# A mixture-of-experts loop, written out, with its matrix products in another order and its weights loaded in runs of 8 KB

## The chip, the cores and the metric

The kernel runs on one core of a Trainium2 chip. The time is device microseconds (us) of one execution, and the median of several runs is compared.

## What is computed

One layer of a hybrid model over two groups of 128 tokens (256 tokens of 1024 features in all, everything in float32). A token mixer (attention, a gated recurrence, a gated MLP) comes first; then every token goes through 4 of 32 experts:

```python
logits = hf @ wr + br;  top_v, top_i = top_k(logits, 4);  gates = softmax(top_v)
def swiglu_expert(xb, wg, bg, wu, bu, wd, bd):
    gate = minimum(xb @ wg + bg, 7.0)
    up = clip(xb @ wu + bu, -7.0, 7.0)
    glu = gate * sigmoid(1.702 * gate)
    return ((up + 1.0) * glu) @ wd + bd
out[t] = sum over the 4 experts e of token t: gates[t, e] * swiglu_expert(h[t], e)
```

Each expert has three 1024 x 1024 matrices (gate, up, down), 12.6 MB together, so the loop over the 32 experts reads 403 MB of weights once.

## The kernel before

It is written with explicit engines and semaphores: each engine runs its own list of instructions, and waits stand where the author wrote them.

**Weights.** SyncE loads all large weights through one ring of 12 slots of 1 MB (`ring`, each 128 partitions x 2048 floats). A slot is loaded again when TensorE has counted it as used (`chunks_used`). An expert is 12 chunks, four to a matrix, so the ring holds just one expert. A chunk is 256 rows of a matrix; partition p holds rows p and 128 + p of it, that is two runs of 4 KB. `load_expert` stands in a hardware loop over the experts.

**One expert on TensorE** (the loop at line 1480, two experts to a turn). `product(B[0], 0, ...)` opens the bank with the bias (line 1424, 32 rows of `pick` against `mbias`) and adds 16 pairs of matmuls (line 1431): the stationary operand is 64 token slots, the moving one 512 columns of weights, and the two halves of the 1024 columns go to the two halves of one bank. `combine` (line 1441) adds the previous expert's stored rows `ysb`, scaled by `gT`, into four banks. `spread` (line 1406) broadcasts the next expert's ranks and gates over the partitions for VectorE, which makes `gT` of them (lines 998, 1001). `product(B[1], 1, ...)` is the up product. `gather` (line 1415) multiplies the token rows by a 0/1 matrix `Ptok` into the 64 slots of the next expert. `down` transposes the activations (line 1454) and waits for ScalarE's copy of them (line 623) before the down product (line 1431 too, from `k_pool`).

**VectorE** clips the gate (`gate_step`, line 1005), prepares the next expert's routing (`route`, `slot_gates`), and after the up product makes the activation (`up_step`, lines 1009 to 1013). **ScalarE**, in this order: the sigmoid (line 619), the copy of the gathered tokens out of its bank (line 615), the copy of the transposed activations (line 623), the copy of the down product's rows (line 625).

Ahead of the loop stand the router and, on TensorE, matmuls that only keep it at work (`keep_clock`, line 1134), the first spread and gather, and `open_sums` (line 1463), which starts the four result banks with the gates times the down bias. The normed rows are made on VectorE at lines 934 and 940 and transposed at line 1368.

An expert has 64 slots. If more than 64 tokens choose it, later rounds follow behind a branch; a list of them is made at line 1471.

Of the kernel before, what the change touches and what calls it, by code (L numbers as in the profile page):

```python
# [20 lines left out]
ALU = mybir.AluOpType  # L21
# [37 lines left out]
AT_MOE = AT_MODG2 + 4  # L59
WOUT = [2, 3, 0, 1]  # L60
# [4 lines left out]
C_SLOTCOL = C_SLOTROW + CAP  # L65
C_THR, C_E, C_OFF = C_SLOTCOL + 1, C_SLOTCOL + 2, C_SLOTCOL + 3
C_IOTA = C_SLOTCOL + 4
# [4 lines left out]
def shape_constants():  # L72
# [9 lines left out]
    f[:, C_SLOTROW:C_SLOTROW + CAP] = np.arange(1, CAP + 1)  # L82
    f[:, C_SLOTCOL] = i % CAP + 1
# [18 lines left out]
def hybrid_layer(nc, x_prompt, x_sample, cache_k, cache_v, state_hgrn_fwd, state_hgrn_bwd, c, c_ctx,  # L102
# [6 lines left out]
    with ctx:  # L109
# [116 lines left out]
        mbias = moe_pool[0:NE, :].rearrange("p (m n) -> p m n", m=3)  # L226
# [4 lines left out]
        ab = d_pool[:, 0:512]  # L231
        ysb = d_pool[:, 512:1024]
        xe = at_pool[:, 0:512].rearrange("p (k s) -> p k s", k=KT)
        gT = at_pool[:, 512:1024].rearrange("p (b t) -> p b t", b=2)
        pick = cumT[0:NE, 0, 0:256].rearrange("p (b m) -> p b m", b=2)
        Ptok = keyT[:, 0, 0:2 * CAP].rearrange("p (t s) -> p t s", t=2)
# [13 lines left out]
        rgT = cumT[0:NE, 1, :]  # L250
        zeros = zcol.to_broadcast([P, P])
        identE = wsT[0:NE, 0, 0:NE + 1]
# [33 lines left out]
        def expert_slot(cidx):  # L286
            return (AT_MOE + cidx) % RING

        def chunk_loads(cidx, e):

            return ((AT_MOE + cidx) // RING + 1 + e) * 16

        def used(cidx, e):

            return e * RING + (AT_MOE + cidx + 1)

# [22 lines left out]
        def _(sp):  # L319
# [36 lines left out]
            def load_expert(e, count):  # L356

                for cidx in range(RING):
                    w = (w_gate, w_up, w_down)[cidx // 4]
                    sp.wait_ge(chunks_used, used(cidx - RING, count))  # L360
                    sp.dma_start(ring[:, expert_slot(cidx), :].rearrange("p (k n) -> p k n", k=2),
                                 w[0, bass.ds(e, 1), 256 * (cidx % 4):256 * (cidx % 4 + 1), :]
                                 .rearrange("a (k p) n -> p (a k) n", p=P)).then_inc(slot_loaded[expert_slot(cidx)], 16)

            with sp.Fori(0, NE) as e:
                load_expert(e, e)
            sp.wait_ge(ev("over_list"), 1)
            n_over = sp.value_load(small_i[0:1, 16:17], min_val=0, max_val=MAX_OVER)
            with sp.If(n_over > 0):
                with sp.Fori(0, MAX_OVER) as j:  # L370
                    with sp.If(n_over > j):
                        e = sp.value_load(small_i[0:1, bass.ds(j, 1)], min_val=0, max_val=NE - 1)
                        load_expert(e, j + NE)
# [9 lines left out]
        def _(pool):  # L383
# [28 lines left out]
            small_load("mixer_loaded", rw, router_w[0].rearrange("(k p) e -> p k e", p=P))  # L412
# [18 lines left out]
            for d, out in enumerate((new_sf, new_sb)):  # L431
                pool.dma_start(out.rearrange("b l h k v -> k (b l h) v"),
                               state_out[0:HD, 256 * d:256 * (d + 1)].rearrange("k (h v) -> k h v", h=RH)).then_inc(ev("caches_stored"), 16)
            nc.gpsimd.memset(identE, 0.0).then_inc(ev("idE_zero"), 1)
            pool.wait_ge(ev("idE_zero"), 1)
            nc.gpsimd.affine_select(out=identE, in_=identE, compare_op=ALU.not_equal, fill=1.0, base=0,
                                    pattern=[[-1, NE + 1]], channel_multiplier=1).then_inc(ev("idE_ready"), 1)
# [5 lines left out]
            for m, src in enumerate((b_gate, b_up, b_down)):  # L443
                small_load("mbias_loaded", mbias[:, m, :], src[0])
# [5 lines left out]
        def _(act):  # L450
# [158 lines left out]
            act.wait_ge(ev("rgT_ps"), 1)  # L609
            nc.scalar.copy(rgT, B[1][0:NE, :]).then_inc(ev("rgT_ready"), 1)  # L610

            def tokens_out(count):

                act.wait_ge(ev("xe_ps"), count + 1)
                nc.scalar.copy(xe.rearrange("p k s -> p (k s)"), B[3]).then_inc(ev("xe_ready"), 1)  # L615
# [5 lines left out]
            def down_steps(count):  # L621
                act.wait_ge(ev("aT_ps"), count + 1)
                nc.scalar.copy(aT.rearrange("p c s -> p (c s)"), B[2]).then_inc(ev("aT_ready"), 1)  # L623
                act.wait_ge(chunks_used, used(11, count))
                nc.scalar.copy(ysb, B[2]).then_inc(ev("y_sb"), 1)  # L625

            act.wait_ge(ev("mixer_freed"), 1)
            tokens_out(0)
            with act.Fori(0, NE) as e:
                sigmoid_step(e)  # L630
                tokens_out(e + 1)
                down_steps(e)
            act.wait_ge(ev("over_list"), 1)
            n_over = act.value_load(small_i[0:1, 16:17], min_val=0, max_val=MAX_OVER)
            with act.If(n_over > 0):
                with act.Fori(0, MAX_OVER) as j:
                    with act.If(n_over > j):
                        tokens_out(j + (NE + 1))
                        sigmoid_step(j + NE)
                        down_steps(j + NE)  # L640
# [12 lines left out]
        def _(dve):  # L653
# [265 lines left out]

            dve.wait_ge(ev("caches_stored"), 48)  # L920
            for t in range(2):
# [12 lines left out]
                V.tensor_tensor(rows[:, t, :], xres[:, t, :], gsc, ALU.mult).then_inc(ev("rows_scaled"), 1)  # L934

            for t in range(2):
# [3 lines left out]
                V.scalar_tensor_tensor(rows[:, t, :], rows[:, t, :], rs2[:, t:t + 1], shf, ALU.mult, ALU.add).then_inc(ev("h2_ready"), 1)  # L940
# [7 lines left out]
            V.memset(ysb, 0.0).then_inc(ev("y_sb"), 1)  # L948
# [33 lines left out]
            def route(e, buf, off=None):  # L982

                V.tensor_copy(pick[:, buf, :], identE[:, bass.ds(e, 1)].to_broadcast([NE, P]))
                for t in range(2):
                    r = rank[:, t, bass.ds(e, 1)]
                    if off is None:
                        ins = V.tensor_scalar(Ptok[:, t, :], cst[:, C_SLOTROW:C_SLOTROW + CAP], r, None, ALU.is_equal)
                    else:
                        ins = V.tensor_scalar(Ptok[:, t, :], cst[:, C_SLOTROW:C_SLOTROW + CAP], off, r, ALU.add, ALU.is_equal)  # L990
                ins.then_inc(ev("route_ready"), 1)

            def slot_gates(count, buf, off=None):

                dve.wait_ge(ev("bc_ps"), count + 1)
                scol = cst[:, C_SLOTCOL:C_SLOTCOL + 1]
                if off is None:
                    ch.step(V.tensor_scalar(gT[:, buf, :], B[3][:, 0:256], scol, None, ALU.is_equal))
                else:
                    ch.step(V.tensor_scalar(gT[:, buf, :], B[3][:, 0:256], off, scol, ALU.subtract, ALU.is_equal))  # L1000
                V.tensor_tensor(gT[:, buf, :], gT[:, buf, :], B[3][:, 256:512], ALU.mult).then_inc(ev("gT_ready"), 1)

            def gate_step(count):
                dve.wait_ge(chunks_used, used(3, count))
                V.tensor_scalar(actb, B[0], LIMIT, None, ALU.min).then_inc(ev("gate_min"), 1)  # L1005

            def up_step(count):
                dve.wait_ge(chunks_used, used(7, count))
                V.tensor_scalar(upb, B[1], -LIMIT, LIMIT, ALU.max, ALU.min).then_inc(ev("up_clip"), 1)  # L1009
                dve.wait_ge(ev("up_clip"), count + 1)  # L1010
                ch.step(V.scalar_tensor_tensor(upb, upb, 1.0, actb, ALU.add, ALU.mult))
                dve.wait_ge(ev("gate_sig"), count + 1)
                V.tensor_tensor(ab, upb, sigb, ALU.mult).then_inc(ev("a_ready"), 1)

            dve.wait_ge(ev("idE_ready"), 1)
            dve.wait_ge(ev("rank_ready"), 1)
            route(0, 0)
# [4 lines left out]
            V.tensor_scalar(onehot, cst[:, C_IOTA:C_IOTA + 16], posn, flag, ALU.is_equal, ALU.mult).then_inc(ev("onehot_ready"), 1)  # L1022
# [509 lines left out]
```

## Time and profile before

| what | value |
|---|---|
| three runs | 1286.82 us median, 1284.38 to 1287.12 |
| span of the profiled execution, first to last instruction | 1284.3 us |
| TensorE matmul busy | 1223.1 us, 95% of the span |
| VectorE, ScalarE busy | 250.6 us, 183.5 us |
| read from memory | 453 MB, 354 GB/s over the span |

The profiled execution is shown by its span alone; its own time is not given beside it. The span lies 2.5 us below the median of the runs. Matmuls are pipelined, so that TensorE's busy time is not TensorE at its peak.

### The profile page before, as it was taken

To read this page: it belongs to the slowest core of one execution; us is meant where nothing else is said; L and a number is where in the kernel's file an instruction comes from. 1 tells how busy PE (TensorE), PEld (TensorE's weight loads), DVE (VectorE), ACT (ScalarE), POOL (GpSimd) and SP (SyncE) were. 2 spreads that over 40 slices of the span, in tenths; PEclk is the share of its full clock that TensorE was granted. 3 is DMA by queue.
4 is the path that set the end of the run, shared out by engine and by line. 5 is a ranking of instruction groups with operands and counts; after the bars stand their busy time and mean duration, and the time that the engine had idled before them with its cause. 6 is when DMAs were issued, how large, how long until landed. Compare 5 with 4: busy or idle time off the path is not lost.

```text
span 1284.3 us, 15147 instructions
## 1 busy us (share of the span) xinstructions
PE 1223.1 (95%) x6020; PEld 552.0 (43%) x6020; DVE 250.6 (20%) x535; ACT 183.5 (14%) x305; POOL 19.8 (2%) x40
## 2 busy tenths in 40 slices
PE   6699999999999999999999999999999999999995
PEld 1388965543333334443333333333333333333332
DVE  1334571511111111111111111111111111111113
ACT  1122431201111111111111111111111111111111
POOL 3000000000000000000000000000000000000000
PEclk9599999969999999999999999999999999999998
DMA  9994359529999999999999999999999999999971
GB/s 316 333 331 140 118 202 360 197 110 373 398 407 406 406 407 405 403 409 408 405 407 406 405 408 403 405 404 410 405 404 408 407 406 406 407 408 406 405 303 33
DMA packets 135160, 455.34 MB, mean 355 GB/s; under 512 B 7967, under 2 KB 21299, under 8 KB 135014
## 3 DMA queue, kind: packets, MB, share of 16 engines
q1 hardware_dynamic: 132080, 446.73, 89.3%
q0 software_dynamic: 2064, 6.98, 1.6%
q10 hardware_dynamic: 998, 1.37, 0.4%
q8 instruction: 13, 0.21, 0.1%
q14 instruction: 5, 0.04, 0.0%
HBM read 453.35 MB, written 1.70 MB: 354 GB/s over the span
## 4 chain that ended last, share of the span: by engine, by line
PE 82%; ACT 3%; DVE 1%; issue 0%
PE bank L1431 53%; PE bank L1415 10%; PE bank L1424 5%; PE bank L1441 5%; PE bank L1406 3%; PE bank L1307 2%; ACT k_pool L623 1%; PE bank L1102 1%; ACT at_pool L615 1%; PE bank L1134 1%; PE bank L1109 1%; PE bank L1463 0%; PE bank L1375 0%; PE bank L1343 0%; DVE xres L1063 0%; DVE k_pool L1062 0%
## 5 line engine op out<-in xcount | busy, mean ns | idle before, releaser
L1431 PE MATMUL bank<-ring,at_pool 128*64 128x512 f32 x2048 | 456.1, 598 | 0.0
L1431 PEld LDWEIGHTS bank<-ring,at_pool 128*64 128x64 f32 x2048 | 141.9, 137 | 310.5 <-issue 310.5
L1431 PE MATMUL bank<-ring,k_pool 128*64 128x512 f32 x1024 | 226.8, 595 | 23.0 <-ACT k_pool L623 23.0
L1431 PEld LDWEIGHTS bank<-ring,k_pool 128*64 128x64 f32 x1024 | 70.7, 137 | 158.5 <-issue 127.9
L1415 PEld LDWEIGHTS bank<-keyT,rows 128*128 128x128 f32 x1056 | 123.7, 196 | 28.6 <-issue 28.6
L1005 DVE TENSOR_SCALAR k_pool<-bank 128x512 f32<-128x512 f32 x32 | 22.1, 692 | 578.9 <-PE bank L1431 578.9
L1415 PE MATMUL bank<-keyT,rows 128*128 128x64 f32 x1056 | 128.5, 281 | 0.0
L615 ACT COPY at_pool<-bank 128x512 f32<-128x512 f32 x33 | 19.3, 586 | 443.3 <-PE bank L1415 443.3
L1424 PE MATMUL bank<-kv_pool,cumT 32*64 32x512 f32 x256 | 69.6, 620 | 0.0
L1009 DVE TENSOR_SCALAR k_pool<-bank 128x512 f32<-128x512 f32 x32 | 22.1, 692 | 226.9 <-PE bank L1431 226.9
L1441 PE MATMUL bank<-d_pool,at_pool 64*128 64x512 f32 x264 | 65.6, 615 | 0.7 <-ACT d_pool L625 0.7
L1152 PE MATMUL bank<-colsT,ring 128*128 128x256 f32 x224 | 51.7, 392 | 0.8 <-DVE colsT L718 0.8
L619 ACT ACTIVATE k_pool<-k_pool 128x512 f32<-128x512 f32 x32 | 20.1, 629 | 224.7 <-DVE k_pool L1005 224.7
L625 ACT COPY d_pool<-bank 128x512 f32<-128x512 f32 x32 | 18.8, 586 | 230.0 <-PE bank L1431 230.0
L1152 PEld LDWEIGHTS bank<-colsT,ring 128*128 128x128 f32 x224 | 43.9, 198 | 8.0 <-DVE colsT L718 1.2
L1155 PE MATMUL bank<-ring,colsT 128*128 128x256 f32 x192 | 43.4, 380 | 0.0
L1441 PEld LDWEIGHTS bank<-d_pool,at_pool 64*128 64x128 f32 x264 | 22.7, 186 | 43.1 <-issue 41.5
L619 ACT ACT_TABLE_LOAD x32 | 41.1, 1283 | 0.6
L1102 PE MATMUL bank<-ring,condT 128*32 128x512 f32 x192 | 29.4, 747 | 11.2 <-DMA ring<-in_w_mod 11.2
L1155 PEld LDWEIGHTS bank<-ring,colsT 128*128 128x128 f32 x192 | 35.7, 190 | 4.6
L1406 PE MATMUL bank<-cumT 32*128 32x512 f32 x66 | 37.0, 640 | 0.0
L1424 PEld LDWEIGHTS bank<-kv_pool,cumT 32*64 32x64 f32 x256 | 12.4, 131 | 50.9 <-issue 50.9
(300 smaller groups left out, 590.5 us busy)
## 6 DMA issues: line engine op xcount, KB each, us to landing
ring<-in_w_gate SPq DMA_DIRECT2D x128, 1024.0 KB, 9.5
ring<-in_w_up SPq DMA_DIRECT2D x128, 1024.0 KB, 8.7
ring<-in_w_down SPq DMA_DIRECT2D x128, 1024.0 KB, 7.4
ring<-in_w_mod SPq DMA_DIRECT2D x24, 1024.0 KB, 10.1
ring<-in_w_in SPq DMA_DIRECT2D x13, 1024.0 KB, 12.5
ring<-in_w_out SPq DMA_DIRECT2D x4, 1024.0 KB, 6.7
k_pool<-in_const_masks POOLq DMA_DIRECT2D x1, 1024.0 KB, 8.0
g<-in_b_mod POOLq DMA_DIRECT2D x2, 512.0 KB, 12.3
```

The costliest lines, as they stand in the source:

```text
L615: nc.scalar.copy(xe.rearrange("p k s -> p (k s)"), B[3]).then_inc(ev("xe_ready"), 1)
L619: nc.scalar.activation(sigb, actb, ACT.Sigmoid, scale=ALPHA).then_inc(ev("gate_sig"), 1)
L1005: V.tensor_scalar(actb, B[0], LIMIT, None, ALU.min).then_inc(ev("gate_min"), 1)
L1102: ins = mm(B[mod_bank(n)][32 * j:32 * (j + 1), :], condT[:, 4 * r + j, :], w[:, j, :], start=r == 0, stop=r == 1, tile_position=(0, 32 * j))
L1152: ins = mm(bank[:, 256 * r:256 * (r + 1)], w[:, k, P * r:P * (r + 1)], hT[:, k, :, :], start=k == 0, stop=k == KT - 1)
L1155: ins = mm(bank[:, 256 * r:256 * (r + 1)], hT[:, k, r, :], w[:, k, :], start=k == 0, stop=k == KT - 1)
L1307: ins = mm(B[2 * t + half], catT[:, 2 * WOUT[i] + kk, t, :], w[:, kk, 512 * half:512 * (half + 1)], start=i == 0 and kk == 0, stop=i == 3 ...
L1406: mm(B[3], pick[:, buf, :], rgT, start=True, stop=True).then_inc(ev("bc_ps"), 1)
L1415: ins = mm(B[3][:, CAP * k:CAP * (k + 1)], rows[:, t, P * k:P * (k + 1)], Ptok[:, t, :], start=t == 0, stop=t == 1)
L1424: mm(bank[CAP * half:CAP * (half + 1), :], pick[:, buf, 0:CAP], mbias[:, m, cols], start=True, stop=False)
L1431: ins = mm(bank[CAP * half:CAP * (half + 1), :], lhsT(2 * r + kk), w[:, kk, 512 * half:512 * (half + 1)], start=m == 2 and r == 0 and kk = ...
L1441: ins = mm(B[4 + 2 * t + half], gT[r, buf, P * t:P * (t + 1)], ysb[r, :], start=False, stop=False)
```

## The change

- The loops of all engines over the experts are written out; no register counts experts.
- On TensorE an expert e is now: up product of e, combine of e - 1, gate product of e + 1, transposes of e's activations, gather of the tokens of e + 2, down product of e, two transposes that turn the gates of e's slots (`Pgate`) into `gT`. The chunks come through the ring in that order (`at_moe`).
- `spread`, `pick`, `rgT` and the identity `identE` go. VectorE compares a row of slot numbers with the rank of each token (`pick_tokens`, `pick_gates`, which multiplies by the gate too) and copies the transposed result out (`gates_out`).
- The gathered tokens `xe` have two buffers; `gT` has one.
- The gate is multiplied with its sigmoid ahead of the up step (`glu_step`), and the up step's last operation is split in two that write the columns in another order.
- The three biases stand on partitions 0 to 95 of one zeroed tile, and the bias matmul takes a column of the identity, broadcast, over all 128 partitions.
- A chunk's 256 rows are laid out so that partition p holds rows 2p and 2p + 1, one run of 8 KB. For this the normed rows (lines 934 and 940), the router's weights and the activations are kept in the matching order; the operation of line 940 becomes four.
- `open_sums` follows the first down product.

```diff
-            def load_expert(e, count):
...
-            with sp.Fori(0, NE) as e:
-                load_expert(e, e)
+            def load_rows(view, w, e, r):
+                return sp.dma_start(view.rearrange("p (k n) -> p k n", k=2),
+                                    w[0, bass.ds(e, 1), 256 * r:256 * (r + 1), :].rearrange("a (p k) n -> p (a k) n", p=P))
...
+            load_matrix(GATE, 0)
+            for e in range(NE):
+                load_matrix(UP, e)
+                if e + 1 < NE:
+                    load_matrix(GATE, e + 1)
+                load_matrix(DOWN, e)
...
             act.wait_ge(ev("mixer_freed"), 1)
-            tokens_out(0)
-            with act.Fori(0, NE) as e:
-                sigmoid_step(e)
-                tokens_out(e + 1)
-                down_steps(e)
+            tokens_out(0, 0)
+            tokens_out(1, 1)
+            sigmoid_step(0)
+            for e in range(NE):
+                act_transposed(e)
+                if e + 1 < NE:
+                    sigmoid_step(e + 1)
+                if e + 2 < NE:
+                    tokens_out(e + 2, e % 2)
+                rows_out(e, at_moe(DOWN, e) + 4)
...
-                V.tensor_tensor(rows[:, t, :], xres[:, t, :], gsc, ALU.mult).then_inc(ev("rows_scaled"), 1)
+                V.tensor_tensor(rows_out_of(t), pairs(xres[:, t, :]), pairs(gsc), ALU.mult).then_inc(ev("rows_scaled"), 1)
...
-                V.scalar_tensor_tensor(rows[:, t, :], rows[:, t, :], rs2[:, t:t + 1], shf, ALU.mult, ALU.add).then_inc(ev("h2_ready"), 1)
+                for r in range(4):
+                    block_r = rows[:, t, 256 * r:256 * (r + 1)]
+                    ins = V.scalar_tensor_tensor(block_r, block_r, rs2[:, t:t + 1],
+                                                 shf[:, 256 * r:256 * (r + 1)].rearrange("p (m k) -> p k m", k=2), ALU.mult, ALU.add)
+                ins.then_inc(ev("h2_ready"), 1)
...
+            def pick_gates(e):
+
+                for t in range(2):
+                    ins = V.tensor_scalar(Pgate[:, t, :], slot_no, rank[:, t, e:e + 1], gate[:, t, e:e + 1],
+                                          ALU.is_equal, ALU.mult)
+                ins.then_inc(ev("pg_ready"), 1)
...
-            with dve.Fori(0, NE // 2) as i:
-                ch.enter(i, 4)
-                for u in range(2):
-                    e = i * 2 + u
-                    gate_step(e)
-                    dve.wait_ge(ev("xe_ps"), e + 1)
-                    route(e + 1, 1 - u)
-                    slot_gates(e + 1, 1 - u)
-                    up_step(e)
-            ch.leave(NE // 2)
+            dve.wait_ge(ev("xe_ps"), 1)
+            pick_tokens(1)
+            gate_step(0, at_moe(GATE, 0) + 4, later=False)
+            for e in range(NE):
+                if e + 2 < NE:
+                    dve.wait_ge(ev("xe_ps"), e + 2)
+                    pick_tokens(e + 2)
+                if e:
+                    dve.wait_ge(ev("gT_ps"), e)
+                pick_gates(e)
+                glu_step(e)
+                up_step(e, at_moe(UP, e) + 4)
+                if e + 1 < NE:
+                    gate_step(e + 1, at_moe(GATE, e + 1) + 4)
+                gates_out(e)
...
-            with pe.Fori(0, NE // 2) as i:
-                for u in range(2):
-                    e = i * 2 + u
-                    pe.wait_ge(ev("xe_ready"), e + 1)
-                    product(B[0], 0, u, xe_tile, e)
-                    combine(1 - u, e + 1)
-                    spread(1 - u, e + 1)
-                    product(B[1], 1, u, xe_tile, e)
-                    gather(e + 1)
-                    down(u, e)
-            combine(1, NE + 1)
+            product(B[0], GATE, 0, tokens(0), main_rows)
+            gather(1)
+            for e in range(NE):
+                product(B[1], UP, e, tokens(e), main_rows)
+                if e:
+                    combine(e - 1)
+                if e + 1 < NE:
+                    pe.wait_ge(ev("xe_ready"), e + 2)
+                    pe.wait_ge(ev("gate_min"), e + 1)
+                    product(B[0], GATE, e + 1, tokens(e + 1), main_rows)
+                act_transpose(e)
+                if e + 2 < NE:
+                    gather(e + 2)
+                pe.wait_ge(ev("aT_ready"), e + 1)
+                product(B[2], DOWN, e, a_tile, main_rows)
+                if e + 2 < NE:
+                    pe.wait_ge(ev("xe_ready"), e + 3)
+                if e == 0:
+                    pe.wait_ge(ev("gateT_ready"), 1)
+                    open_sums()
+                gate_transpose(e)
+            combine(NE - 1)
```

## Rows read from the trace of the kernel before

**Rows 1.** The page: span, busy times, and TensorE's clock in 40 slices.
```profile
span 1284.3 us, 15147 instructions
...
PE 1223.1 (95%) x6020; PEld 552.0 (43%) x6020; DVE 250.6 (20%) x535; ACT 183.5 (14%) x305; POOL 19.8 (2%) x40
...
PEclk9599999969999999999999999999999999999998
```

**Rows 2.** The chain of waits, from 600 to 700 us: start, length, what.
```profile
605.05 3.73 PE bank L1415 x32
...
608.80 0.49 ACT at_pool L615
609.29 0.59 ACT k_pool L623
...
609.93 7.09 PE bank L1431 x32
617.01 1.00 PE bank L1424 x4
618.02 7.02 PE bank L1431 x32
625.04 1.92 PE bank L1441 x8
626.95 1.05 PE bank L1406 x2
...
640.90 7.09 PE bank L1431 x32
```

**Rows 3.** The transfers, from 400 to 1200 us: 40 slices; queue with packets, MB, share.
```profile
GB/s 409 404 409 406 403 410 400 409 410 406 399 412 405 403 411 403 409 409 403 409 405 405 410 402 407 410 403 398 412 406 406 409 404 409 405 406 410 406 402 410
...
q1 hardware_dynamic: 84310, 325.06, 102.1%
```

**Rows 4.** SyncE's waits over the span: total us, times, longest.
```profile
SPq L361 <- PE bank L1431: 782.9, 372, 40.3
```

**Rows 5.** VectorE in the timeline from 600 to 640 us: start, length, what.
```profile
605.10 0.69 DVE L1009 TENSOR_SCALAR k_pool<-bank 128x512 f32<-128x512 f32 x1 [7.09 <-PE bank L1431]
```

**Rows 6.** The chain of waits, from 228 to 310 us.
```profile
239.94 0.89 PE bank L1368 x8
...
254.24 1.82 PE bank L1134 x4
...
260.15 3.60 PE bank L1415 x16
263.75 3.71 PE bank L1463 x4
...
272.88 1.90 PE bank L1424 x4
274.78 9.51 PE bank L1431 x32
```

**Rows 7.** Line 784 on VectorE, at all seven strides: ns min, median, max.
```profile
L784 DVE TENSOR_TENSOR gain<-d_pool,hq_hi x28: 408/422/438, 106.2 to 167.3; 64x256 f32<-64x256 f32 x28
```

**Rows 8.** Stretches: length, busy (count) of PE, PEld, DVE, ACT, POOL, clock, DMA, GB/s.
```profile
200.00:230.00 30.00, 30.00 (x100) 15.61 (x99) 2.08 (x3) 1.72 (x4) 1.47 (x3) 1.00 0.84 310
259.40:279.90 20.50, 20.50 (x57) 10.40 (x58) 0.00 (x0) 1.87 (x2) 0.00 (x0) 0.50 0.01 2
```

**Rows 9.** Line 940 on VectorE, in the timeline from 228 to 245 us.
```profile
238.40 1.28 DVE L940 SCALAR_TENSOR_TENSOR rows<-rows,small,shf 128x1024 f32<-128x1024 f32 x1
```

**Rows 10.** The timeline from 1254 us to the end.
```profile
1267.57 0.59 ACT L625 COPY d_pool<-bank 128x512 f32<-128x512 f32 x1 [7.19 <-PE bank L1431]
...
1268.21 1.99 PE L1441 MATMUL bank<-d_pool,at_pool 64*128 64x512 f32 x8 [0.69 <-ACT d_pool L625]
```

**Rows 11.** The transfers, from 75 to 80 us, while rows of 1 KB load.
```profile
q1 hardware_dynamic: 1731, 1.74, 110.2%
```

**Rows 12.** The transfers, from 0 to 345 us.
```profile
q8 instruction: 12, 0.20, 0.2%
```

## What I expect, and how the numbers come out

> **What bounds the kernel now.** I read the page first, to see which engine is full. TensorE is busy for 95% of the 1284.3 us and its clock is at the upper level almost throughout [rows 1]. Some 995 of these us, from the first product [rows 6] to the last combine [rows 10], are the loop over 32 experts. There I read the chain of waits over three experts, for what each piece of the loop adds to the path [rows 2]. From one start of the down product to the next (609.93 to 640.90) an expert takes 30.97 us: gate bias 1.00, gate product 7.02, combine 1.92, spread 1.05, up bias 1.00, up product 7.02, gather 3.73, then 1.15 in which TensorE does not lead (608.78 to 609.93: ScalarE copies first the gathered tokens, then the transposed activations), and the down product 7.09. Three of these follow from the program's order: the spread, and the two copies in a row.
>
> Then I asked whether the weights could set this pace. One chunk of the ring is 1.049 MB, an expert takes 12, so 30.97 us ask for 406 GB/s. That is what the queues deliver, with the 16 engines full (102.1%), and single slices reach 409 to 412 [rows 3]. So TensorE and the transfers are close to a tie. SyncE decides it: its loads waited 782.9 us, 372 times, for a product to free a slot [rows 4], and no product in [rows 2] waits for a load. TensorE leads, the transfers follow with little to spare. A change that only shortens TensorE's path has to be measured against the transfers as well.
>
> **The change, part by part.**
>
> *The spread goes* (32 in the loop, 1.05 each): +33.6 us. What replaces it on VectorE (two comparisons with a rank column, then a multiply) stands beside products that last 7 us.
>
> *The order up, combine, gate of the next expert, transposes, gather, down.* The up result is now clipped and multiplied on VectorE while combine and the next gate product run, about 9.9 us of cover for three operations of at most 0.69 each [rows 5]. The four activation transposes go ahead of the gather, so that the 3.73 us gather covers the 0.59 us copy, and the tokens gathered are those of the expert after next, with two buffers, so their copy has the whole down product as cover. Without that cover the 1.15 us would stay. What enters TensorE's path is the transposes themselves: eight such transposes take 0.89 us [rows 6], so four take 0.44. Per expert 1.15 - 0.44 = 0.71, for the 30 experts that still have a gather to hide behind: +21.3 us.
>
> *The gate transposes*, two per expert after the down product: 32 x 0.22 = -7.0 us. Their copy (256 columns, 0.42 us by [rows 7]) lies beside the next up product. Nothing after them on TensorE waits for VectorE before combine, 8 us later.
>
> *Fewer rounds.* Before, the loop gathers once for an expert that does not exist and combines once on zeros: +3.7 and +1.9.
>
> *Bias.* Still two matmuls of 512 columns, now over 128 partitions instead of 32. Phases cost more than their matmuls: four bias instructions take 1.00 where the product needs 0.22 for one (32 in 7.02), so some 0.12; combine, eight in 1.92, some 0.17 [rows 2]. If the bias now flows into its product, 64 x 0.15 = 9.6 us are gained; if each new transpose group pays such a change, 62 x 0.15 = 9.3 us are lost. I take zero for both, and both ends go into the range.
>
> *The start.* Between 256.06, the end of a keep-alive, and the first product (274.78) TensorE ran a spread, list matmuls, the opened sums in two halves (the second 3.71), a gather in two halves (3.60 for one) and another keep-alive [rows 6], with the clock at 0.50, that is 1.2 of 2.4 GHz, from about 259.4 to 279.9 [rows 8]. Now the gather comes at once (3.73, its end at the lower clock: 3.8), then the list (six small matmuls at the 0.11 that a transpose takes, doubled for the clock: about 1.0), a wait for the token copy and the list (about 1.0, by the 0.59 of a copy and its signals), bias 1.90, then the product, which I leave at its 9.51: it ends near 273.2 instead of 284.29, +11.1. The opened sums move behind the first down product, at the upper clock: 8 x 0.455 (four such matmuls take 1.82) = -3.6. The router's rows are now written in pairs. Strides cost VectorE nothing here: one operation at seven strides stays within 408 to 438 ns [rows 7]. But a 1.28 us operation [rows 9] becomes four of a quarter, about -0.3. Start: +7.1. Bounds: gather and first product wholly at the lower clock (3.5 and 4.5 more) take it to about -1; no drop of the clock gives +10.
>
> *The end.* Combine waited 0.64 us from its last product to the stored rows [rows 10]. Now a transpose pair and a 0.42 copy come first, about 0.1 longer: -0.1.
>
> Sum: 33.6 + 21.3 - 7.0 + 3.7 + 1.9 + 7.1 - 0.1 = 60.5, so the span of 1284.3 becomes 1223.8. The profiled execution shows only its span; the median of the runs is 2.5 us above it, so 1226.
>
> *The transfers.* The new expert takes 30.97 - 1.05 - 0.71 + 0.22 = 29.4 us, which asks for 428 GB/s, more than 406. Two things speak for it all the same. First, the ring starts full. From the first freed slot (about 267) 372 chunks have to arrive before the last down chunk is used, 19 us before the end of the span (14.1 of them follow the last combine), at 1205. Allowing 3 us of early waits, the transfers may take (1205 - 270) / 372 = 2.513 us a chunk, 417 GB/s; before it was 2.56 at the slices' 410. Second, the 8 KB runs. Rows of 1 KB fill the engines at 1.74 MB in 5 us, 348 GB/s [rows 11], 47.1 ns a packet on 16 engines; 4 KB rows at 410 take 159.8. That is 37.6 ns per KB and 9.5 fixed, so 8 KB would take 310 ns: 423 GB/s, 2.48 us a chunk, an estimate beyond the measured sizes. The transfers would then be done 12 us before they bind. The bounds are 2.48 and, where the longer run gains nothing, 2.56.
>
> The Trainium skill (DMA: Bandwidth & Descriptors, "Why small descriptors are slow (HBM only)") gives a fixed cost of about 3 cycles beside one cycle for each 32 bytes of a packet. By that rule, scaled to 410 GB/s at 4 KB, 1 KB rows would run at 384 GB/s; the trace has 348, so here the fixed cost is larger than the page's, and the rows decide.
>
> *The written-out loop.* The period is the same across the loop's jump and inside it, so the jump cost TensorE nothing and its removal gains nothing. What is new is code to fetch: 12 blocks came in the first 345 us at 0.2% of 16 engines, about 1 us each [rows 12], while TensorE was busy 30.00 of 30.00 us with the transfers at 0.84 [rows 8]. I cost the fetches at nothing. The Trainium skill (Runtime: NRT & Kernel Launch, "Instruction fetch mechanics") says that code streams in ahead in sequence and that a jump breaks this; the trace agrees with the first and shows no cost of the second.
>
> **The rivals.**
>
> *The transfers set the pace* (chance 0.20). For it: they are full already, and the longer run may gain nothing, or still be sent as two packets of 4 KB, so that this part of the change does not do what it says. Against it: the full ring at the start, and the rate that rises from 1 to 4 KB. At 2.56 us a chunk (372 x 2.56 = 952, done at 1222 instead of 1205) the time is 1244.
>
> *They do so only just* (0.08). If joining two packets saves 4 ns of the 9.5 worked out above, 8 KB take 315.6 ns, a chunk (8 packets on each engine) 2.525 us, and the transfers bind by (2.525 - 2.513) x 372 = 4.5 us: 1231. This is about what the page's rule named above would make of it.
>
> *Long runs are slower* (0.04, the other side). If a partition's 8 KB, or the order in which memory is read, takes the stream below 392 GB/s, 2.675 us a chunk, the transfers end 60 us later than they may and the kernel is slower than before; at 380 GB/s it is about 1320. Nothing in [rows 3, 11] points there: the rate rises with the run.
>
> *Code starves TensorE* (0.04). At the rate of [rows 12] it is one block per 29 us, so one per expert; at 1 us, or at twice that, and hidden by nothing, it costs 32 to 64 us: 1258 to 1290.
>
> *The clock stays low at the start or falls in the loop* (0.07): 8 us, the bounds of the start, to some 20, as long as the stretch of [rows 8] was, so 1234 to 1246.
>
> **How the numbers follow.** TensorE sets the time, as summed, 0.61: 1226, by its bounds 1214 to 1243. The range takes in the transfer case at 2.56 and the lower bound of the bias: 1216 to 1246. Runs of this kernel differ by 0.2%, so less is no change. All cases but the long runs and the worst of the code fetch are faster by far: 0.93 faster, 0.02 same, 0.05 slower.
>
> **What would show it.** No spread; the down product starting right where the gather ends; the token copy inside the down product; 29.4 us from one down product to the next; about 423 GB/s or the queue idle at times; the first product ending near 273. Wrong: products that wait for ring loads, late in the loop above all (then the transfers bind); gaps on TensorE that nothing releases (code); a period beyond 29.8 with no wait (phase changes); a second stretch at the lower clock.

## The result, and the profile after

The changed kernel takes 1229.74 us, median of four runs (1227.88 to 1230.50), against 1285.60 for the kernel before (1282.69 to 1287.12). The ratio is 0.9564, with a 95% interval of 0.9548 to 0.9581: 4.4% faster. The forecast was 1226 in a range of 1216 to 1246. The profiled execution took 1229.05 us with a span of 1227.2, 57.1 us below the span before; the sum had said 60.5.

The total came out close. The page of the changed kernel shows that its parts did not:

```profile
PE 1178.6 (96%) x5974; PEld 546.0 (44%) x5974; DVE 256.9 (21%) x567; ACT 142.9 (12%) x273; POOL 20.2 (2%) x39
...
q8 instruction: 48, 0.79, 0.3%
...
PE 60%; DMA 22%; DVE 2%; SPq 1%; issue 0%; ACT 0%; DVEq 0%
...
ring<-in_w_gate SPq DMA_DIRECT2D x128, 1024.0 KB, 20.5
```

The page of the kernel before has for the last two:

```profile
PE 82%; ACT 3%; DVE 1%; issue 0%
...
ring<-in_w_gate SPq DMA_DIRECT2D x128, 1024.0 KB, 9.5
```

Read the third line: 22% of the chain that ended last is now waiting for a load of expert weights, where the page before names none. And a chunk lands some 21 us after its issue instead of 7 to 10: loads now stand in a queue for most of a period.

In the middle of the loop TensorE still leads. The chain of waits there, start and length of each piece, answers to [rows 2]:

```profile
617.18 3.52 PE bank L1447 x32
620.70 7.02 PE bank L1471 x32
627.72 0.37 PE bank L1502 x2
628.09 1.01 PE bank L1466 x4
629.09 6.87 PE bank L1471 x32
635.96 1.92 PE bank L1482 x8
637.88 1.01 PE bank L1466 x4
638.89 6.87 PE bank L1471 x32
645.75 0.59 PE bank L1495 x4
646.34 3.52 PE bank L1447 x32
649.86 5.29 PE bank L1471 x23
```

From down product to down product (620.70 to 649.86) it is 29.16 us, and there is nothing in it but TensorE (the last line is cut off by the end of the window). The down product starts where the gather ends. Later this is no longer so. A table by stretches (time, PE, PEld, DVE, ACT, POOL busy, granted clock, DMA share, GB/s) shows it:

```profile
268.00:300.00 32.00, 32.00 (x182) 15.82 (x180) 4.77 (x10) 4.20 (x6) 0.00 (x0) 1.00 0.95 376
300.00:340.00 40.00, 40.00 (x194) 15.89 (x192) 6.16 (x16) 2.87 (x5) 0.00 (x0) 1.00 0.98 392
...
600.00:800.00 200.00, 200.00 (x1034) 83.56 (x1032) 29.06 (x66) 15.40 (x27) 0.00 (x0) 1.00 1.01 421
800.00:1000.00 200.00, 198.18 (x1002) 78.93 (x999) 29.94 (x70) 14.29 (x25) 0.00 (x0) 1.00 1.01 421
1000.00:1150.00 150.00, 147.43 (x747) 58.93 (x745) 21.00 (x50) 11.43 (x20) 0.00 (x0) 1.00 1.01 421
1150.00:1200.00 50.00, 46.81 (x228) 16.99 (x228) 6.34 (x14) 3.99 (x7) 0.00 (x0) 1.00 1.00 416
...
1200.00:1204.00 4.00, 3.28 (x16) 1.19 (x16) 1.61 (x3) 0.58 (x1) 0.00 (x0) 1.00 0.53 223
1204.00:1208.00 4.00, 4.00 (x22) 1.42 (x20) 0.00 (x0) 0.00 (x0) 0.00 (x0) 1.00 0.19 78
```

The transfers run full at 421 GB/s from 340 on. TensorE is busy 200.00 of 200 us until 800 and loses 7.6 us between 800 and 1200, and that is a lower bound, since matmuls that arrive singly still count as busy. The waits say to what (engine, line, what it waited for: us, times, longest):

```profile
PEld bank L1471 <- DMA ring<-in_w_up: 21.9, 27, 1.4
...
PEld bank L1471 <- DMA ring<-in_w_gate: 13.8, 22, 1.4
```

PEld is TensorE's own loading of its stationary operand. Its waits partly stand beside running matmuls, so their sum is more than TensorE lost. SyncE's own waits for a freed slot fell from the 782.9 us, 372 times, of [rows 4] to 697.2, 349 times. Full slots, then a queue that is never empty, then a ring that runs dry: the transfers set the end after all, by a little.

### The profile page after: what moved, and what is told of

It reads as the page before. It is cut to its first block, busy times and chain, and to the rows that moved or that the text cites. A ratio compares the mean times of both kernels' runs of the same rounds, so it can differ in the third digit from the quotient of the medians.

```text
span 1227.2 us, 13618 instructions
## 1 busy us (share of the span) xinstructions
PE 1178.6 (96%) x5974; PEld 546.0 (44%) x5974; DVE 256.9 (21%) x567; ACT 142.9 (12%) x273; POOL 20.2 (2%) x39
## 4 chain that ended last, share of the span: by engine, by line
PE 60%; DMA 22%; DVE 2%; SPq 1%; issue 0%; ACT 0%; DVEq 0%
PE bank L1471 39%; DMA ring<-in_w_up 22%; PE bank L1447 7%; PE bank L1466 4%; PE bank L1482 4%; PE bank L1347 2%; PE bank L1495 1%; PE bank L1142 1%; PE bank L1502 1%; SPq L352 1%; PE bank L1174 0%; PE bank L1149 0%; PE bank L1415 0%; PE bank L1511 0%; PE bank L1383 0%
## 5 line engine op out<-in xcount | busy, mean ns | idle before, releaser
L1471 PEld LDWEIGHTS bank<-ring,at_pool 128*64 128x64 f32 x2048 | 145.7, 137 | 306.1 <-issue 270.3
L1447 PE MATMUL bank<-d_pool,rows 128*128 128x64 f32 x1024 | 118.0, 273 | 0.0
L1447 PEld LDWEIGHTS bank<-d_pool,rows 128*128 128x128 f32 x1024 | 116.9, 192 | 1.3 <-issue 1.3
L626 ACT COPY k_pool<-bank 128x512 f32<-128x512 f32 x32 | 18.7, 585 | 579.0 <-PE bank L1495 579.0
L1019 DVE COPY cumT<-bank 128x256 f32<-128x256 f32 x32 | 13.6, 424 | 346.2 <-PE bank L1502 346.2
L1466 PE MATMUL bank<-kv_pool,cst 128*64 128x512 f32 x256 | 69.4, 620 | 0.7 <-DVE small_i L1054 0.7
L1482 PE MATMUL bank<-d_pool,cumT 64*128 64x512 f32 x256 | 63.6, 615 | 0.6 <-DVE cumT L1019 0.6
L1482 PEld LDWEIGHTS bank<-d_pool,cumT 64*128 64x128 f32 x256 | 22.1, 186 | 41.0 <-issue 40.2
L1038 DVE SCALAR_TENSOR_TENSOR kv_pool<-k_pool 128x256 f32<-128x256 f32 x64 | 33.9, 611 | 3.3
L1347 PE MATMUL bank<-ring,colsT 128*128 128x512 f32 x64 | 27.9, 593 | 0.0
```

Source lines behind the costliest of these rows:

```text
L1038: ins = V.scalar_tensor_tensor(ab[:, cols].rearrange("p (k m) -> p m k", k=2), upb[:, cols].rearrange("p (m k) -> p m k", k=2), 1.0, actb[ ...
L1347: ins = mm(B[2 * t + half], catT[:, 2 * WOUT[i] + kk, t, :], w[:, kk, 512 * half:512 * (half + 1)], start=i == 0 and kk == 0, stop=i == 3 ...
L1447: ins = mm(B[3][:, CAP * k:CAP * (k + 1)], rows[:, t, P * k:P * (k + 1)], Ptok[:, t, :], start=t == 0, stop=t == 1)
L1466: mm(bank[CAP * half:CAP * (half + 1), :], row, mbias[:, 512 * half:512 * (half + 1)], start=True, stop=False)
L1471: ins = mm(bank[CAP * half:CAP * (half + 1), :], lhsT(2 * r + kk), w[:, kk, 512 * half:512 * (half + 1)], start=m == 2 and r == 0 and kk = ...
L1482: ins = mm(B[4 + 2 * t + half], gT[r, P * t:P * (t + 1)], ysb[r, :], start=False, stop=False)
```

## The experiments

The time ahead of the loop moves from run to run: the first gate product of the profiled executions starts anywhere from 270.5 to 274.8 us in the three with the old order and from 255.9 to 267.6 in those with the new one, with stretches at the lower clock that differ in length. So beside the ratio the table has a cleaner number, read in each trace from the chain of waits: from the start of the first gate product to the start of the last combine. For the changed kernel it is the distance between these two lines:

```profile
264.75 8.15 PE bank L1471 x32
...
1211.17 1.99 PE bank L1482 x8
```

| kernel | median us | ratio, 95% | loop us |
|---|---|---|---|
| before | 1285.6 | 1 | 993.4 |
| changed | 1229.74 | 0.9564 [0.9548, 0.9581] | 946.4 |
| old kernel, 8 KB runs | 1283.4 | 0.9998 [0.9974, 1.0021] | 993.1 |
| old kernel, written out | 1285.44 | 0.9995 [0.9981, 1.0009] | 993.4 |
| new order, 4 KB runs | 1250.1 | 0.9719 [0.9692, 0.9747] | 970.5 |
| changed, lighter down chunks | 1216.48 | 0.9461 [0.9435, 0.9488] | 933.8 |
| changed, late transposes | 1241.53 | 0.9654 [0.9627, 0.9680] | 958.8 |
| changed, writes in row order | 1228.16 | 0.9559 [0.9536, 0.9582] | 945.6 |
| changed, ring of 10 | 1231.91 | 0.9570 [0.9543, 0.9596] | 951.7 |
| runs of 16 KB | 1216.23 | 0.9460 [0.9434, 0.9486] | 935.6 |

The ratios go by runs of the kernel before that were taken beside each group: 1285.17 us (4 KB runs, old kernel with 8 KB runs, lighter chunks, late transposes) and 1286.88 us (the others); the changed kernel's goes by the 1285.60 above.

**The new order with the old 4 KB runs.**

```diff
-     w[0, bass.ds(e, 1), 256 * r:256 * (r + 1), :].rearrange("a (p k) n -> p (a k) n", p=P))
+     w[0, bass.ds(e, 1), 256 * r:256 * (r + 1), :].rearrange("a (k p) n -> p (a k) n", p=P))
...
-     V.tensor_tensor(rows_out_of(t), pairs(xres[:, t, :]), pairs(gsc), ALU.mult)
+     V.tensor_tensor(rows[:, t, :], xres[:, t, :], gsc, ALU.mult)
```

(and the router's weights, the shift and the activations back in plain order)

> The new order with the old layout of the weights (two runs of 4 KB a partition), rows and activations in the old order of columns too. Theory A, the transfers bind in the changed kernel's last third: with packets of 4 KB at some 410 GB/s (2.56 us a chunk instead of 2.487) the 372 chunks end 27 us later, products wait for loads from the first third of the loop on, and the time is about 1256 us. Theory B, TensorE alone sets the pace and the run length is of no account: 1227 to 1230 us, no more waits for loads than in the changed kernel.

1250.1 us, between the two theories and 6 us below that of A; the loop is 24.1 us longer than the changed kernel's. The queue's line over 400 to 1150, and a piece of the chain of waits:

```profile
q1 hardware_dynamic: 79448, 306.29, 102.3%
...
618.26 5.00 PE bank L1471 x23
623.26 18.46 DMA ring<-in_w_gate
```

306.29 MB in 750 us are 408 GB/s, and already at 623 the chain runs through a load. The order alone brings 22.9 us of the loop's 47.0 and the longer run the other 24.1. A chunk of 1.049 MB takes 2.567 us at 408.4 GB/s and 2.495 at the changed kernel's 420.3 (below), 0.072 more, 27 us over 372 chunks. Nearly all that this stream loses shows in the loop.

**The old kernel with 8 KB runs.**

```diff
-     .rearrange("a (k p) n -> p (a k) n", p=P)).then_inc(slot_loaded[expert_slot(cidx)], 16)
+     .rearrange("a (p k) n -> p (a k) n", p=P)).then_inc(slot_loaded[expert_slot(cidx)], 16)
```

(and the rows, the router's weights and the activations in the matching order)

> The kernel before, with the weights in runs of 8 KB and the rows, the router's weights and the activations in the matching order, nothing else. Theory A, TensorE led there with 30.97 us an expert: no gain, 1286 to 1288 us, the 1 to 2 us being the slower scattered writes ahead of the router; the queue idles more. Theory B, the tie with the transfers held the old loop back: 1265 to 1280 us.

No change: 0.9998, and the loop is 993.1 us against 993.4. The queue's line over 400 to 1150:

```profile
q1 hardware_dynamic: 41847, 304.73, 99.5%
```

304.73 MB in 750 us are the 406 GB/s that the kernel before asked for; the share is now below 100% where [rows 3] had 102.1, so the queue idles between loads. Neither part gains alone what it gains with the other: the layout 0, the order 22.9, both 47.0.

**The changed kernel with lighter down chunks.**

```diff
-                    load_rows(ring[:, n % RING, :], (w_gate, w_up, w_down)[m], e, r).then_inc(slot_loaded[n % RING], 16)
+                    if m == DOWN and e:
+                        sp.dma_start(ring[:, n % RING, 0:1024], w_down[0, e, 256 * r:256 * (r + 1), :]
+                                     .rearrange("(p k) n -> p k n", p=P)[:, 0, :]).then_inc(slot_loaded[n % RING], 16)
+                    else:
+                        load_rows(ring[:, n % RING, :], (w_gate, w_up, w_down)[m], e, r).then_inc(slot_loaded[n % RING], 16)
```

> The changed kernel, but from the second expert on only half of each down chunk is loaded (the second row of each pair keeps what the slot held before), which leaves out a sixth of the weights' bytes and so computes something else. TensorE's work is the same. Theory A, the transfers cost the changed kernel about 13 us at the end: no product waits for a load, the period stays 29.16 us, time 1215 to 1218 us. Theory B, what is late at the end is something else (TensorE's own work, code): 1228 to 1230 us.

1216.48 us, the loop 933.8. The stretches late in the loop:

```profile
800.00:1000.00 200.00, 200.00 (x1034) 83.51 (x1032) 30.11 (x70) 16.02 (x28) 0.00 (x0) 1.00 0.93 360
1000.00:1150.00 150.00, 150.00 (x772) 62.08 (x770) 21.51 (x50) 11.44 (x20) 0.00 (x0) 1.00 0.93 360
```

TensorE never waits and the queue idles, and the period is 29.16 us as in the changed kernel, so the lighter loads leave TensorE's own work as it was. So TensorE alone needs 933.8 us for the loop, and the transfers cost the changed kernel 12.6 us. This is the run that shows both halves of what happened.

**The activation transposes behind the gather again.**

```diff
-                act_transpose(e)
                 if e + 2 < NE:
                     gather(e + 2)
+                act_transpose(e)
```

> The changed kernel with the four activation transposes behind the gather again, so that ScalarE's copy of them is no longer covered: the period on TensorE grows from 29.16 to about 29.85 us, 20 us over 30 experts. Theory A, the transfers take 29.84 us an expert, so most of it disappears in waits for loads that are there already: about 1237 us, 7 us more than the changed kernel, with hardly a product waiting for a load. Theory B, TensorE's path simply adds up: about 1250 us.

1241.53 us, the loop 12.4 us longer. The chain of waits:

```profile
622.71 3.71 PE bank L1447 x32
626.42 0.46 PE bank L1495 x4
626.88 0.02 issue
626.90 0.59 ACT k_pool L626
627.50 0.04 issue
627.54 4.50 PE bank L1471 x19
```

Without its cover the copy costs 0.65 us (0.59 and the two issues), and the period is 29.96 instead of 29.16. Thirty times 0.80 on the 933.8 of TensorE alone give 957.8; measured is 958.8. (Theory A, at 1237 us, had the period 0.11 too short.) No product waits for the ring here: TensorE leads again. So 24 us were at stake and only 12.4 show, because the changed kernel already gives 12.6 to the transfers.

**The old kernel, written out.**

```diff
-            with pe.Fori(0, NE // 2) as i:
+            for i in range(NE // 2):
```

(the same for SyncE, ScalarE and VectorE)

> The kernel before with its four expert loops written out and nothing else: same order, same layout. Theory A, the jump cost TensorE nothing and the fetch of the longer code costs nothing: 1283 to 1287 us, period 30.97 us, some 36 code blocks more than before. Theory B, the jump cost something: 1275 to 1282 us. Theory C, code fetched beside the full transfers stalls TensorE: 1290 us or more, gaps that nothing releases.

0.9995, and 993.4 us for the loop in both. Neither the jump nor fetching nearly four times the code (48 blocks for 13) costs anything that shows here. But TensorE leads in this kernel, so the run does not say what the fetches cost a stream that binds.

**VectorE writes in row order and reads at a step of two.**

```diff
             def pairs(ap):
-                return ap.rearrange("p (r m k) -> p r m k", r=4, k=2)
+                return ap.rearrange("p (r m k) -> p r k m", r=4, k=2)
             def rows_out_of(t):
-                return rows[:, t, :].rearrange("p (r k m) -> p r m k", r=4, k=2)
+                return rows[:, t, :].rearrange("p (r k m) -> p r k m", r=4, k=2)
```

(and the same in the up step's last operation)

> The changed kernel with the loop order of three operations on VectorE turned, so that they read in steps and write in a row: the scaled rows ahead of the router and the up step's last operation. Theory A, a scattered write is what made the first take 2.03 us instead of 1.23 and the second 0.61 instead of 0.42, and the first stands on the path to the router: both return to the old times, the router and with it the first product and the first freed slot come 2.2 us earlier, time 1227 to 1228 us. Theory B, any step costs, read or write: durations stay, 1229 to 1230 us.

1228.16 us (1219.39 to 1232.46): the intervals of this ratio and of the changed kernel's overlap, so the time doesn't tell the two apart. The operations do, and for theory A. The changed kernel, then this one (groups of VectorE: busy us, mean ns of one):

```profile
L951 DVE TENSOR_TENSOR rows<-xres,gsc 128x1024 f32<-128x1024 f32 x2 | 4.1, 2026 | 0.2
...
L1038 DVE SCALAR_TENSOR_TENSOR kv_pool<-k_pool 128x256 f32<-128x256 f32 x64 | 33.9, 611 | 3.3
```

```profile
L951 DVE TENSOR_TENSOR rows<-xres,gsc 128x1024 f32<-128x1024 f32 x2 | 2.5, 1228 | 0.2
...
L1038 DVE SCALAR_TENSOR_TENSOR kv_pool<-k_pool 128x256 f32<-128x256 f32 x64 | 24.4, 422 | 3.3
```

A write that jumps 512 bytes from element to element costs 1.65 and 1.45 times as much; the same exchange done on the reading side, at a step of two floats, costs nothing (1228 ns for the first, 1225 in plain order in the 4 KB run). In the loop this stands beside products, hence no gain in the loop (945.6 against 946.4).

**A ring of 10 slots.**

```diff
-RING = 12
+RING = 10
```

> The changed kernel with a ring of 10 slots instead of 12. Theory A, the transfers' end is the first freed slot plus the chunks not yet loaded by then, so the head start counts: two chunks fewer, 2 x 2.487 = 5 us later, about 1235 us, waits for loads from an earlier expert on. Theory B, the ring only has to cover the time from issue to landing and its length is of no account: 1229 to 1230 us.

The median, 1231.91 us, lies between the two theories, 2.2 us above the changed kernel's, and the intervals of the two ratios overlap, so the time does not decide. The traces speak for A: the loop is 951.7 us against 946.4, +5.3, and TensorE's first waits for ring loads come between 700 and 750 us instead of between 850 and 900. Two slots fewer are two chunks less of a lead, 2 x 2.49 = 5.0 us: the stock in the ring at the start is spent once, chunk by chunk, and is worth its transfer time.

**Runs of 16 KB.** On the kernel with row-order writes, four neighbouring rows a partition, a pair of slots filled by one load of 2 MB:

```diff
-                return sp.dma_start(view.rearrange("p (k n) -> p k n", k=2),
-                                    w[0, bass.ds(e, 1), 256 * r:256 * (r + 1), :].rearrange("a (p k) n -> p (a k) n", p=P))
+                return sp.dma_start(view.rearrange("p s (k n) -> p (s k) n", k=2),
+                                    w[0, bass.ds(e, 1), 512 * r:512 * (r + 1), :].rearrange("a (p k) n -> p (a k) n", p=P))
...
-                    ins.then_inc(chunks_used, 1)
+                    ins.then_inc(chunks_used, 2)
```

> The in-row writes, and expert weights in pairs of slots: a partition holds four neighbouring rows, one run of 16 KB, 512 rows to a load, six loads an expert. Theory A, a packet carries a fixed cost of about 8 ns (4 KB: 159.8 ns at 410 GB/s, 8 KB: 311.3 ns at 421 GB/s): 16 KB give about 427 GB/s, the transfers end 11 us earlier and just no longer bind, time 1216 to 1222 us. Theory B, the gain is eaten, by a fixed cost that does not shrink further (rate 421 GB/s) or by the coarser grain, in which a product waits for 2 MB at once: 1227 to 1233 us.

1216.23 us (1213.97 to 1218.48), ratio 0.9460: the best of all, 1.1% below the changed kernel. The queue's line over 400 to 1150, and the longest of its few waits on the expert loads:

```profile
q1 hardware_dynamic: 21975, 320.05, 100.4%
...
PEld bank L1470 <- DMA ring<-in_w_up: 3.5, 3, 2.1
```

Over the whole run PEld waits 6.5 us in all for expert loads, where the changed kernel's waits 41.0. 320.05 MB in 750 us are 427 GB/s, and the loop is 935.6 us, 1.8 above the one in which the transfers don't bind. (Its first gate product ran wholly at the upper clock, 6.87 us instead of the 8.11 of that run, so the transfers still cost some 3.)

## Why the prediction was nearly right, and by which two errors

Against the sum's span of 1223.8 the profiled one is 1227.2, 3.4 more. The sum had the first product end at 273.2, with the router's 0.3 at 273.5, so at 9.51 a product it starts at 264.0; it starts at 264.75, +0.75. The tail behind the start of the last combine is as long as before (16.0 us, 16.1 before). The loop is 946.4 us, where the sum's terms give 943.6 (993.4 - 33.6 - 21.3 + 7.0 - 3.7 - 1.9, and 3.6 for the opened sums, 0.1 for its end): +2.8. That 2.8 is what is left of two errors: TensorE alone needs 933.8, which is 9.8 less than forecast, and the transfers add 12.6 where I took 0. That these two errors nearly cancel is luck.

**Spread, order, gate transposes, rounds: right.** No spread, no copy on the path, 29.16 us a period where 29.4 was worked out.

**The phase changes, taken at zero: the step that failed on TensorE's side.** Its favourable bound was the truth. Bias and product take 1.01 + 6.87 = 7.88 instead of 8.02 [rows 2]: with the bias over 128 partitions the two together are shorter, 64 x 0.14 = 9.0 us of the 9.6 that were its bound; no run changes the bias alone, so that the width is the cause is not tested. The other bound was met only in part. Each new group of transposes is 0.15 dearer than the sum had it (0.59 and 0.37 for 0.44 and 0.22), but the gather behind the first is 0.21 cheaper (3.52 for 3.73) and the down product 0.07. The run with late transposes shows that this belongs to the order: there the gather follows a product directly and takes 3.71, and the transposes 0.46. Together that is some -0.27 a period, 8 us over 30 experts; with 1.4 from a first product of 8.1 instead of 9.51 it is nearly all of the 9.8.

**The transfers, taken at nothing: the step that failed on the other side.** The price of a chunk was nearly right: 315.22 MB in 750 us are 420.3 GB/s for the queue, 2.495 us a chunk where 2.48 was estimated (the 421 and 422 of the stretches hold the code too). What was mis-sized is when the stream runs full and when TensorE needs its end. I had 372 x 2.48 = 923 us from 270, an end near 1193, and a need at 1205. In the trace the stream ends shortly before 1208, 15 us later. The stretches say why: 5.6 us are 372 times the 0.015; 268 to 300 at 376 GB/s costs 3.4 us against 421, and 300 to 340 at 392 another 2.8, where I had allowed 3 for both; and from 1190 to 1208 the falling rate costs 5.7 (0.6, 1.9 and 3.3 by its three stretches, 397, 223 and 78 GB/s). That makes 14.5. The end was the least foreseen. The last loads on SyncE's timeline:

```profile
1174.66 8.52 SPq L352 DMA_DIRECT2D ring<-in_w_down  x4
```

The last is issued at 1183, so from then on all that is left stands in the queues, and yet the share falls to 0.53 and 0.19 before the last bytes land: the 16 engines do not run out together. The packets of the trace, taken one by one, show eight engines that end between 1197.9 and 1201.4 and eight that work on until 1204.6 to 1207.2; from 1202 to 1204 the share is 0.49 and 0.51. In the kernel before all end between 1243 and 1245. A mean rate over the loop does not hold this; what sets the eight back is, as far as this trace shows, the code (see below). The need, in turn, came 9 us earlier, since TensorE was faster (933.8 from 264.75, less the same way from the last down chunk to the last combine, is 1195.6). 15 and 9 against the margin of 12 that the prediction gave: the transfers bind by 12, and the run with lighter chunks measured 12.6. The load that the end really waits for is not the last of the down matrix, by which all this is reckoned, but the last of the up matrix, four chunks earlier:

```profile
1170.02 27.81 DMA ring<-in_w_up
...
1203.11 7.09 PE bank L1471 x32
```

It lands at 1197.83, and the down product behind it runs through in its 7.09 us. TensorE alone needs it 13.1 us ahead of the last combine (in the run with lighter chunks), here at 1185.5: by this load the transfers bind by 12.3. The shares of the 15 are read from one trace; that they are the transfers' at all is what that run shows.

**The rivals.** "The transfers set the pace" was right in its place (waits late in the loop, as the prediction's signs had it) and wrong in its reason, the rate. The nearest price was that of "only just", 1231, whose reason was the rate too. The chances given to the cases add up to 1.04, 0.04 too much. The ring of 10 (+5.3 us), the 4 KB runs (+24.1) and the 16 KB runs (-10.8) all move the loop as a binding stream must. Had TensorE needed what the sum gave it, the transfers would have bound by some 3 us only, and the time would have been much the same: the later of two ends counts, so an error in the earlier one does not show.

**Code, costed at nothing: right for TensorE, wrong for the stream.** The written-out old kernel's loop is as long as the looped one's. But the 0.3% of the engines' time in which 48 blocks came is a mean over 16 engines. Packet by packet, a block of 16 KB holds one engine for 0.97 to 1.11 us, about the 1 us of the prediction, and that engine's next packet of the ring takes some 0.8 us instead of 0.31: some 1.5 us lost. The losses seem to fall on the same eight engines, in turn. The lengths of the blocks repeat in eights (1.07, 1.06, 1.10, 1.10, 1.09, 1.02, 1.02, 1.07 us from 418 on, the same again from 615 on), and set against the bytes moved, the ring's loads land some 1.5 us later from every eighth block on (those at 738.9, 937.6 and 1140.1 us). The 35 blocks from 340 to 1197 are 4.4 for each of the eight, some 6.6 us, and eight engines end 6.4 us behind the others in the mean. A load has landed only when the last engine has its part, so by this estimate about half of the 12.6 us is the code's (the 14.5 above hold it, in the rate and in the end). No run has the new order with its loops kept, so this share is not tested.

**The start: right in its end, not in its parts.** The first product ended at 272.89. The router's path was dearer than the 0.3 of the sum: the rows' scattered write, which I had put at nothing by [rows 7], where the operands are read in steps and the result is written in a row, takes 2.03 us instead of 1.23. From VectorE's first operation on the last projection to the first transposes of the rows are 11.3 us (230.9 to 242.2), with the plain layout 9.9. Against that the gather ran at the upper clock: over 259.4 to 279.9, at 0.50 in [rows 8], the granted clock is now 0.92 on average. The opened sums cost 3.63, as said.

```profile
242.21 1.09 PE bank L1408 x8
...
258.38 3.52 PE bank L1447 x32
...
272.89 3.71 PE bank L1447 x32
...
303.33 3.63 PE bank L1511 x8
...
1210.19 0.38 PE bank L1502 x2
```

**The end: -0.3 instead of -0.1.** From the last product (1210.19) to combine (1211.17) are 0.98 us, 0.64 in [rows 10].

## What to carry to other kernels

When an engine and the transfers are close to a tie, the time is the later of two ends: add up both streams separately to their own last instant, with the stream's start, its first unfull stretches and the uneven end of its queues, and count the fetch of written-out code in the stream, by the engines that carry it and not as a mean of 16. Then test each alone (lighter loads for one, a smaller ring for the other). A layout that shortens transfers gained nothing here while TensorE led, and 24 us once TensorE was shortened, so measure the two together. And put the exchange of elements that a layout needs on the reading side of VectorE, at the smallest step, not on the writing side.

## What the runs showed of the hardware

**The price of a packet is a straight line up to 16 KB.** On 16 engines: 47.1 ns for 1 KB [rows 11], 160 for 4 KB (409 GB/s), 311 for 8 KB (421), 613 for 16 KB (427 to 428). Between any two neighbours it is 37.7 to 37.8 ns a KB, with 9.4 ns fixed. The prediction's estimate, made from the first two, held at sizes two and four times as long.

**VectorE's strides.** With 16 KB runs the reads step by four floats, and the row-order kernel's advantage is gone; groups of VectorE in that kernel:

```profile
L952 DVE TENSOR_TENSOR rows<-xres,gsc 128x1024 f32<-128x1024 f32 x2 | 4.3, 2154 | 0.2
L1037 DVE SCALAR_TENSOR_TENSOR kv_pool<-k_pool 128x512 f32<-128x512 f32 x32 | 34.6, 1081 | 3.3
```

2154 ns where a step of two floats took 1228. So for these two operations a step of 8 bytes is free and one of 16 is not. The Trainium skill (SBUF — State Buffer, "Door 1: The DMA port swizzle (why `[64,N]` ≈ `[32,N]`)") speaks of lines of 16 bytes, of which at least two accesses each are needed for full speed; the two steps agree with that, one access to a line being a step of four floats. Its reckoning beside it, that one may stride over 4 fp32 for free, does not hold for a step of four: 2154 ns is the price here.

**ScalarE's table.** In the kernel with hardware loops the sigmoid's table was loaded in each turn; in the written-out old kernel the same line loads it once. Before, then the old kernel written out:

```profile
L619 ACT ACT_TABLE_LOAD x32 | 41.1, 1283 | 0.6
```

```profile
L619 ACT ACT_TABLE_LOAD x1 | 1.3, 1283 | 0.0
```

These 40 us stood off the path in both, so they cost and gained nothing here.
